# The down projection's last two products: streamed operands with homes of their own, and the last phase bank by bank

## The reference

```python
def conv_ffn(h, w_up, w_conv, b_conv, w_down):
    u = causal_dwconv(h @ w_up, w_conv, b_conv)
    gate, up = jnp.split(u, 2, axis=-1)
    return (jax.nn.silu(gate) * up) @ w_down
...
        x = x + conv_ffn(h, w_up[l], w_ffn_conv[l], b_ffn_conv[l], w_down[l])
    return rmsnorm(x, final_g)
```

## Time and profile before

| | |
|---|---|
| median of 3 runs | 1095.54 us (1094.78 to 1095.6) |
| profiled execution | 1094.99 us |
| its span | 1093.3 us |
| mean granted clock of TensorE | 0.984 |
| PE busy | 1033.3 us (95% of the span) |
| DVE busy | 728.9 us (67%) |
| ACT busy | 500.4 us (46%) |
| last matmul starts | 1086.57 us |

### The profile page before, as it was taken

How to read it: one execution, slowest core, us unless ns; L and a number is a source line. 1 busy time by engine, 2 the same in 40 slices (tenths; PEclk the granted TensorE clock), 3 DMA queues, 4 the chain that set the end, 5 groups by cost and what they waited for, 6 DMA issues and landing times.

```text
span 1093.3 us, 13267 instructions
## 1 busy us (share of the span) xinstructions
PE 1033.3 (95%) x4933; PEld 848.5 (78%) x4933; DVE 728.9 (67%) x1153; ACT 500.4 (46%) x939; POOL 74.6 (7%) x80
## 2 busy tenths in 40 slices
PE   5999999999899998999999999999999999998655
PEld 4888888888788886888888888888888778886434
DVE  5343455641955659797777787777778699865346
ACT  7532435452742225565445454544546344444224
POOL 5011222220410000000000000000000000000000
PEclk9999999999999999999999999999999999999977
DMA  8134111010342242333122232313229960102234
GB/s 217 39 92 122 39 39 40 22 37 20 104 129 78 77 124 70 97 102 110 59 92 81 77 97 77 97 58 105 69 68 388 390 223 1 58 10 67 97 113 157
DMA packets 108640, 107.75 MB, mean 99 GB/s; under 512 B 13330, under 2 KB 81032, under 8 KB 108576
## 3 DMA queue, kind: packets, MB, share of 16 engines
q1 hardware_dynamic: 107040, 103.56, 29.9%
q0 software_dynamic: 1536, 3.34, 1.2%
HBM read 86.93 MB, written 19.96 MB: 98 GB/s over the span
## 4 chain that ended last, share of the span: by engine, by line
PE 83%; DMA 7%; DVE 6%; ACT 2%; issue 1%; SPq 0%; DVEq 0%; POOL 0%; ACTq 0%; POOLq 0%
PE pz L1796 18%; PE pz L2093 7%; PE pz L2094 7%; PE pz L2095 7%; DMA b_raw<-in_w_down 6%; PE pd L2094 5%; PE pd L2095 5%; PE pd L2093 5%; PE pd L2114 3%; PE pd L2116 3%; PE pd L2117 3%; PE pd L2022 3%; PE pd L2024 3%; PE pd L2023 3%; DVE d_lo L1650 2%; PE pz L2114 2%
## 5 line engine op out<-in xcount | busy, mean ns | idle before, releaser
L1004 ACT ACTIVATE ws_hi<-raw 128x512 fp32r<-128x512 f32 x88 | 52.9, 626 | 107.4 <-PE pz L2095 51.7
L1796 PE MATMUL pz<-h_hi,w_hi 128*128 128x512 f32 x304 | 99.2, 399 | 2.7 <-DVE h_lo L1189 2.6
L2093 PE MATMUL pz<-ht_hi,ws_hi 128*128 128x512 f32 x240 | 94.2, 393 | 5.3 <-DVE u L1583 5.3
L1796 PE MATMUL pz<-h_lo,w_hi 128*128 128x512 f32 x304 | 96.7, 391 | 0.0
L1796 PE MATMUL pz<-h_hi,w_lo 128*128 128x512 f32 x304 | 96.3, 389 | 0.0
L2114 PE MATMUL pd<-d_hi,d_hi 128*128 128x512 f32 x176 | 72.0, 409 | 24.3 <-DVE d_lo L1650 24.3
L2094 PE MATMUL pz<-ht_lo,ws_hi 128*128 128x512 f32 x240 | 93.9, 391 | 0.0
L2095 PE MATMUL pz<-ht_hi,ws_lo 128*128 128x512 f32 x240 | 93.8, 391 | 0.0
L2093 PE MATMUL pd<-ht_hi,ws_hi 128*128 128x512 f32 x200 | 77.8, 389 | 0.0
L2094 PE MATMUL pd<-ht_lo,ws_hi 128*128 128x512 f32 x200 | 77.8, 389 | 0.0
L2095 PE MATMUL pd<-ht_hi,ws_lo 128*128 128x512 f32 x200 | 77.8, 389 | 0.0
(11 more groups left out here) (287 smaller groups left out, 2368.9 us busy)
## 6 DMA issues: line engine op xcount, KB each, us to landing
raw<-in_w_up SPq DMA_DIRECT2D x48, 512.0 KB, 4.9
act_rows<-gate SPq DMA_DIRECT2D x22, 512.0 KB, 2.7
a<-act_rows SPq DMA_DIRECT2D x33, 256.0 KB, 6.4
b<-in_w_down SPq DMA_DIRECT2D x33, 256.0 KB, 9.0
b_raw<-in_w_down SPq DMA_DIRECT2D x33, 256.0 KB, 3.6
raw<-in_w_in SPq DMA_DIRECT2D x14, 512.0 KB, 3.7
a_raw<-act_rows SPq DMA_DIRECT2D x22, 256.0 KB, 3.3
x_in<-in_x SPq DMA_DIRECT2D x8, 512.0 KB, 6.0
```

The lines of the kernel that those rows point to most:

```text
L1004: nc.scalar.activation(ws_hi[m][:, :, :], summand(p, i), ACT.Copy).then_inc(s["ws_hi_made"], 1)
L1796: ins = mm(dst[:, h * HALF:(h + 1) * HALF], w[:, c], v[:, h * HALF:(h + 1) * HALF], start=first, stop=last)
L2093: mm(dst, wh[:, k, :], xh[:, k, :], start=begins and k == 0, stop=False, skip_group_check=not begins)
```

## The change

Product 4's second operand (B21) gets eleven places, `b21`: the three `a_raw`, the three `b_raw` and the last five `b11`. The first six are loaded once all of product 2 is split, the others once the tile's step of product 7 is split. Product 3's operands (A12 and B22) are loaded into `a21[k]` and `b12[k]`, whose contents are done with when step `(5, k)` is split. The high and low parts of the last phase swap their halves of the slots, so that the low part is written over its own source. `S4` waits on the semaphores of the A21 loads, `T4` on those of the stream and on `tile_loaded[0]`. `KEEP` becomes 11: the whole last phase goes bank by bank, and in bank 0 PE waits for each step's split in turn instead of for all. The four `y_add` of phase 5 move out of DVE's loop and stand right behind it.

```diff
@@ -56,7 +56,7 @@
 STEPS = len(DOWN_ORDER) * KT
 RING = 4
 STREAM_RING = 3
-KEEP = 5
+KEEP = KT
 LAST = STEPS - KT
 
 
@@ -77,12 +77,9 @@
 A21_GROUP = (0, 0, 0, 1, 1, 1, 1, 2, 2, 2, 2)
 
 
-STREAMS = [(2, _k) for _k in range(KT)] + [(4, _k) for _k in range(KT)] + [(3, _k) for _k in range(KT)]
-STREAM_COUNT = {}
-_loads = [0] * STREAM_RING
-for _n, (_p, _k) in enumerate(STREAMS):
-    _loads[_n % STREAM_RING] += 16 if _p == 4 else 32
-    STREAM_COUNT[(_p, _k)] = _loads[_n % STREAM_RING]
+def a21_total(k, times):
+
+    return 32 * times * A21_GROUP.count(A21_GROUP[k])
 
 
 SUMS = {2: ("T1", "T2"), 6: ("S1", "S2"), 7: ("T3", "S3"), 4: ("T4",), 3: ("S4",)}
@@ -236,12 +233,17 @@
         b12, b22 = halves("b12", B12_SLOTS, 0), halves("b22", B12_SLOTS, 2048)
         a21, a22 = halves("a21", A21_SLOTS, 0), halves("a22", A21_SLOTS, 2048)
         a_raw, b_raw = halves("a_raw", STREAM_SLOTS, 0), halves("b_raw", STREAM_SLOTS, 2048)
+        b21 = [*a_raw, *b_raw, *b11[6:]]
         s3 = [at(50, f"s3_{m}", [HALF], extra=2048 * m) for m in range(2)]
         d_hi, d_lo = {}, {}
-        for m, pair in enumerate((*RING_SLOTS, *zip(A21_SLOTS, B12_SLOTS))):
+        for m, pair in enumerate(RING_SLOTS):
             for u in range(2):
                 d_hi[m, u] = at(pair[u], f"d_hi{m}_{u}", [HALF], F32R)
                 d_lo[m, u] = at(pair[u], f"d_lo{m}_{u}", [HALF], F32R, extra=2048)
+        for k, pair in enumerate(zip(A21_SLOTS, B12_SLOTS)):
+            for u in range(2):
+                d_lo[RING + k, u] = at(pair[u], f"last_lo{k}_{u}", [HALF], F32R)
+                d_hi[RING + k, u] = at(pair[u], f"last_hi{k}_{u}", [HALF], F32R, extra=2048)
         x_whole = {mn: at(n, f"x_whole{n}", [4, HALF]) for mn, n in (((0, 0), 42), ((1, 0), 44), ((1, 1), 46))}
         x_block = {mn: [w[:, t, :] for t in range(4)] for mn, w in x_whole.items()}
         x_block[0, 1] = [at(n, f"x12_{t}", [HALF], extra=2048)[:, :] for t, n in enumerate(A11_SLOTS[:4])]
@@ -387,9 +389,9 @@
 
         def down_source(p, k):
 
-            u = STREAMS.index((p, k)) % STREAM_RING if (p, k) in STREAM_COUNT else 0
+            u = k % STREAM_RING
             return {1: (a11[k], b11[k]), 2: (a_raw[u], b_raw[u]), 6: (a11[k], b22[k]), 7: (s3[k % 2], b11[k]),
-                    5: (a21[k], b12[k]), 4: (a22[k], b_raw[u]), 3: (a_raw[u], b_raw[u])}[p]
+                    5: (a21[k], b12[k]), 4: (a22[k], b21[k]), 3: (a21[k], b12[k])}[p]
 
         def added_to(ph):
 
@@ -535,17 +537,27 @@
                 sp.dma_start(a21[k][:, :], act_d[k * P:(k + 1) * P, HALF:]).then_inc(done, 16)
                 sp.dma_start(a22[k][:, :], act_d[(KT + k) * P:(KT + k + 1) * P, HALF:]).then_inc(done, 16)
 
-            def load_stream(p, k):
-                n = STREAMS.index((p, k))
-                u = n % STREAM_RING
-                if n >= STREAM_RING:
-                    sp.wait_ge(s["down_split"], 2 * down_step(*STREAMS[n - STREAM_RING]) + 2)
-                if p != 4:
-                    act_ready(KT + k)
-                    sp.dma_start(a_raw[u][:, :], act_d[(KT + k) * P:(KT + k + 1) * P, 0:HALF])\
-                      .then_inc(stream_loaded[u], 16)
-                h = slice(HALF, D) if p == 3 else slice(0, HALF)
-                sp.dma_start(b_raw[u][:, :], w_down_d[:, KT + k, h]).then_inc(stream_loaded[u], 16)
+            def load_stream(k):
+                u = k % STREAM_RING
+                if k >= STREAM_RING:
+                    sp.wait_ge(s["down_split"], 2 * down_step(2, k - STREAM_RING) + 2)
+                act_ready(KT + k)
+                sp.dma_start(a_raw[u][:, :], act_d[(KT + k) * P:(KT + k + 1) * P, 0:HALF]).then_inc(stream_loaded[u], 16)
+                sp.dma_start(b_raw[u][:, :], w_down_d[:, KT + k, 0:HALF]).then_inc(stream_loaded[u], 16)
+
+            def load_b21(k):
+                if k < 6:
+                    sp.wait_ge(s["down_split"], 2 * down_step(2, KT - 1) + 2)
+                else:
+                    sp.wait_ge(s["down_split"], 2 * down_step(7, k) + 2)
+                done = stream_loaded[k % STREAM_RING] if k < 6 else tile_loaded[0]
+                sp.dma_start(b21[k][:, :], w_down_d[:, KT + k, 0:HALF]).then_inc(done, 16)
+
+            def load_last(k):
+                done = a21_loaded[A21_GROUP[k]]
+                sp.wait_ge(s["down_split"], 2 * down_step(5, k) + 2)
+                sp.dma_start(a21[k][:, :], act_d[(KT + k) * P:(KT + k + 1) * P, 0:HALF]).then_inc(done, 16)
+                sp.dma_start(b12[k][:, :], w_down_d[:, KT + k, HALF:]).then_inc(done, 16)
 
             for i in range(FT - 1):
                 if i + 2 < FT:
@@ -575,7 +587,7 @@
             sp.wait_ge(s["product_done"], len(PRODUCTS))
             store_act(FT - 1)
             for k in range(STREAM_RING):
-                load_stream(2, k)
+                load_stream(k)
             for k in range(3):
                 load_a21(k)
             for i in range(NT // 2):
@@ -586,10 +598,10 @@
                 rows = x1_d[m * HALF:(m + 1) * HALF, half * HALF:(half + 1) * HALF]
                 sp.dma_start(block_[:, :, :], rows.rearrange("(t p) c -> p t c", p=P)).then_inc(s["x1_loaded"], 16)
             for k in range(STREAM_RING, KT):
-                load_stream(2, k)
+                load_stream(k)
                 load_a21(k)
-            for k in range(STREAM_RING):
-                load_stream(4, k)
+            for k in range(6):
+                load_b21(k)
             sp.wait_ge(s["down_split"], 2 * down_step(7, 5) + 2)
             sp.wait_ge(s["y_added"], 1)
             for t in range(4):
@@ -597,10 +609,10 @@
             for half in range(2):
                 sp.dma_start(final_gb[half][:, :], final_g[half * HALF:(half + 1) * HALF].partition_broadcast(P))\
                   .then_inc(s["final_g_loaded"], 16)
-            for k in range(STREAM_RING, KT):
-                load_stream(4, k)
+            for k in range(6, KT):
+                load_b21(k)
             for k in range(KT):
-                load_stream(3, k)
+                load_last(k)
             for n, i in enumerate((4, 5, 6, 7, 0, 1, 2, 3)):
                 for half in range(2):
                     c = slice(half * HALF, (half + 1) * HALF)
@@ -1057,8 +1069,10 @@
                 m = down_place(n)
                 if p == 1:
                     act.wait_ge(tile_loaded[A11_GROUP[k]], 16 + 32 * A11_GROUP.count(A11_GROUP[k]))
-                elif p in (2, 3):
-                    act.wait_ge(stream_loaded[STREAMS.index((p, k)) % STREAM_RING], STREAM_COUNT[(p, k)])
+                elif p == 2:
+                    act.wait_ge(stream_loaded[k % STREAM_RING], 32 * (k // STREAM_RING + 1))
+                elif p == 3:
+                    act.wait_ge(a21_loaded[A21_GROUP[k]], a21_total(k, 2))
                 if p in (3, 4, 5, 6, 7):
                     act.wait_ge(s["down_summed"], SUM_COUNT[({6: "S2", 7: "S3", 5: "S2", 4: "T4", 3: "S4"}[p], k)])
                 if n == 1:
@@ -1613,7 +1627,6 @@
                     .then_inc(s["act_made"], 1)
 
             def down_sum(name, k):
-                u = k % STREAM_RING
                 if name == "T1":
                     g = B12_GROUP[k]
                     dve.wait_ge(b12_loaded[g], (16 if g < 2 else 0) + 32 * B12_GROUP.count(g))
@@ -1622,7 +1635,7 @@
                     dve.wait_ge(s["down_summed"], SUM_COUNT[("T1", k)])
                     args = (b22[k], b22[k], b12[k], ALU.subtract)
                 elif name == "S1":
-                    dve.wait_ge(a21_loaded[A21_GROUP[k]], 32 * A21_GROUP.count(A21_GROUP[k]))
+                    dve.wait_ge(a21_loaded[A21_GROUP[k]], a21_total(k, 1))
                     args = (a21[k], a21[k], a22[k], ALU.add)
                 elif name == "S2":
                     dve.wait_ge(s["down_summed"], SUM_COUNT[("S1", k)])
@@ -1635,11 +1648,15 @@
                 elif name == "T3":
                     args = (b11[k], b22[k], b11[k], ALU.subtract)
                 else:
-                    p = 4 if name == "T4" else 3
-                    u = STREAMS.index((p, k)) % STREAM_RING
-                    dve.wait_ge(stream_loaded[u], STREAM_COUNT[(p, k)])
-                    args = (b_raw[u], b_raw[u], b22[k], ALU.subtract) if p == 4 else \
-                        (a_raw[u], a_raw[u], a11[k], ALU.subtract)
+                    if name == "S4":
+                        dve.wait_ge(a21_loaded[A21_GROUP[k]], a21_total(k, 2))
+                    elif k < 6:
+                        u = k % STREAM_RING
+                        dve.wait_ge(stream_loaded[u], 32 * len(range(u, KT, STREAM_RING)) + 32)
+                    else:
+                        dve.wait_ge(tile_loaded[0], 16 + 32 + 16 * (KT - 6))
+                    args = (a21[k], a21[k], a11[k], ALU.subtract) if name == "S4" else \
+                        (b21[k], b21[k], b22[k], ALU.subtract)
                 dst, x, y, op = args
```

(7 more changed lines are left out.)

## The result

The changed kernel takes 1057.04 us in the median (1056.53 to 1057.89), against 1095.57 us for the kernel before in the same set. The ratio is 0.9648 with a 95% interval of 0.9631 to 0.9665, so it is faster by 38.5 us. The prediction was 1058.0 us. A second measurement beside other kernels gave 0.9655 (0.964 to 0.967). The profiled execution took 1057.3 us, with a span of 1055.6.

The account below looks back on a forecast made before the run. PE was busy 95% of the span, but load round trips over three buffers paced phases 5 and 6. The last split 45.0 us earlier, less 7.3 us behind it, gave 1057.3 us; 0.7 for the clock made 1058.0, range 1053 to 1063.

Parts of the forecast that it names:

- The loads: Products 4 and 3 (phases 5 and 6): loads issued early and hidden, so the last split is done 45.0 us earlier.
- Phase 5 and DVE's pace: Phase 5 takes 29.9 us at PE's 2.72 us a step; then DVE sets the last phase's pace, 1.81 us with `S4`.
- The bank order: Last phase on PE: 102 matmuls remain behind the last split instead of 60, giving back 7.3 us.
- the slower rival: Last phase: the last split comes no earlier, so only the bank order's 7.3 us shows, 1102.8 us; chance 0.04.
- The clock: PE's granted clock while bank 0 waits for splits: at most one fall, costing 0 to 2.0 us, 0.7 taken.
- The upper bound: Clock term: ten matmuls at 0.43 rather than 0.23 us behind 1071.01 us in the old profile, 2.0 us.
- The 1059.3 us that went with the rule: Whole kernel: the time if the skill's warning holds that short idle times make the clock fall; 1057.3 us without it.
- The moved additions and the tail: Phase 5's four additions, left among the last splits, would add 2.4 us; tail unchanged, 6.3 us from last addition to end.
- the sum's 1057.3 us: Whole kernel: 1055.6 us of span plus 1.7 us around it, before the clock term.
- The rival of a longer spell at half clock: Bank 0 of the last phase: clock falls more or longer, 1061.3 us; chance 0.08, shared with a slower DVE pace.
- the starved 6.5 us: Bank 0 of the last phase: PE waits for DVE's splits from about 1019.5 to 1026 us, with holes between steps.

Follow-up runs that it names:

- banks_only: The kernel before with all eleven steps of the last phase bank by bank and a wait per split, loads still streamed through three buffers; 1103.01 us, ratio 1.0083.
- ring_pace: The changed kernel with each load of product 3 held back until the split three steps earlier, as with three buffers; 1091.89 us, ratio 0.9972.
- late11: The changed kernel with each load of product 3 issued eleven steps later, behind product 4's split of the same tile; 1057.51 us, ratio 0.9663.
- p4_streamed: The changed kernel with product 4's operand again streamed through three buffers, its later loads queued behind product 3's; 1065.81 us, ratio 0.9739.
- after_again: The changed kernel itself, nothing altered, measured again in the third set beside other kernels; 1057.57 us, ratio 0.9655.
- adds_in_loop: The changed kernel with the four additions of phase 5 back among the splits of the last phase; 1060.4 us, ratio 0.9684.
- homes_only: The changed kernel with the last phase of the kernel before: `KEEP` = 5, one wait for all splits, additions in the loop; 1051.95 us, ratio 0.9612.

## Why the prediction was right

**The loads (45.0 us).** Right. The last split is done at 1025.15 us instead of 1070.95, 45.8 us earlier. Of that 0.7 us is from before the change's stage: phase 5 begins at 984.62 us instead of 985.34, which I don't put down to the change, since kernels with the same code up to there differ as much among themselves: the last left split of product 7 starts at 947.04 us before, at 946.30 in the changed kernel, and between 945.0 and 948.0 in its variants that differ from it only behind that point. In banks_only, whose code is that of the kernel before up to there, it starts at 944.42. What is left is 45.1 us. ring_pace and late11 show the mechanism by the time of issue, p4_streamed that the two phases add up.

**Phase 5 and DVE's pace.** Right: 29.92 us for the phase, 1.806 us for a step of the last phase, first hole of PE at 1018.8 us (1019.5 counted, less the 0.7).

**The bank order (+7.3 us).** Right as a net figure, within 0.8 us. From the last split to the last matmul it is 1048.87 - 1025.15 = 23.7 us against 15.6, so 8.1 us, of which 0.8 are the clock. But the slower rival took this 7.3 us for the price with late loads, and there that was mis-sized: the 15.6 us before held 2.2 us of cold clock, which stay when the loads are late. The price there is 42 matmuls, 9.5 us; the profile of banks_only has 9.2.

**The clock (0 to 2.0 us, 0.7 taken).** The profiled execution had one fall. The stretches of 5 us put it from about 1023.1 to 1026.5 us (0.81 and 0.85 are 1.9 and 1.5 us at half), and 101 intervals took 23.43 us against 22.89 at full rate. Step 76 begins 0.2 us late, since PE is still at half clock with step 75, and with that the cost is 0.8. The upper bound's reading was slightly off: nine matmuls, not ten, start from 1071.01 us to 1075.02, and the whole spell cost 2.2 us. In the second profile of the same kernel (after_again) the clock did not fall:

```profile
1020.00:1025.00 5.00, 3.09 (x11) 1.60 (x11) 5.00 (x9) 2.61 (x5) 0.00 (x0) 1.00 0.00 0
```

So this term is zero or one fall per execution, and two profiles do not say how often. The Trainium skill (TensorE: Matmul & The Clock Gate, section A second HAM failure mode: psum-queue depth-cycling) lets the clock go down and up under frequent short idle times between groups of matmuls. The section HAM oscillation, which the prediction names, tells of longer waits for loads. Here there was one fall in one profile and none in the other. The 1059.3 us that went with the rule lies above all measured times of the kernel, the highest of which is 1058.57 us.

**The moved additions and the tail.** Right: 2.4 us when left in place, nothing when behind the splits, 6.3 us of tail as before.

**The forecast.** The mechanism and the terms came out as counted, each within 1 us. That the profiled execution took exactly the sum's 1057.3 us is luck: a start of phase 5 that was 0.7 us early and a clock that cost 0.8 cancel. The forecast of 1058.0 us is 1.0 above the median of 1057.04, less than what the interval leaves open. The rival of a longer spell at half clock came in neither profile of the changed kernel; adds_in_loop, with longer holes, had one.

**What the prediction lacked.** It named the starved 6.5 us and said that other banks' matmuls could run there, but did not work out what that is worth against leaving `KEEP` alone. It is 4.7 us by measurement (homes_only; 12% of the gain). PE's work from the start of the last phase is 131 x 0.2266 = 29.7 us, and the changed kernel took 1048.87 - 1014.54 = 34.3, 4.6 us more.

## What to carry to other kernels

When a stage waits for loads, ask first what lets each load be issued. A ring of buffers turns the whole round trip into a period, here 3.9 us for one load and 5.4 us for two against 2.7 us of work, while the same transfers into places that fall free a phase earlier cost nothing. When the operands come from an engine that is slower than one bank's share of the work (1.8 against 0.68 us a step) and faster than all four banks' (2.72), keep PE on all banks until the splits are through, and go bank by bank only for as many steps as the tail needs (five were enough here, with two the last addition came 1.8 us late). Time a two-part change by its parts: one part here gave 43 us and the other took 4.7 back.

## What was not expected of the hardware

The granted clock fell to half behind holes of 0.40, 0.84 and 0.84 us in one execution of the changed kernel, and stayed at 1.00 in another (after_again) with holes of 0.39, 0.83, 0.84, 0.24 and 0.24 us, and in late11 with holes of 0.40, 0.84, 0.84, 0.24 and 0.23 us. late11 is the same program in this stretch. In the kernel before, the holes just ahead of its falls were 3.46 and 2.33 us and 2.42 us (ended by the matmul at 1053.42 us); one more fall lies within the wait of 13.31 us. So with holes of the same lengths the clock fell in one execution and not in two others, and no run here shows what decides it. The one fall cost 0.8 us.
